# Where a two-layer encoder kernel makes its precomputed weight sums

## The reference, cut to what matters

```python
# layer 0 (even): neighbourhood attention heads || convolution channels
h = rmsnorm(x);  z = h @ w_in_e                      # q k v g_a u_a u_b g_b
a = neighbourhood_attention(q, k, v, rpb) * silu(g_a)          # 8 heads
u = conv31(u_a * sigmoid(u_b)) + dw_b
u = silu(layernorm(u)) * silu(g_b)
x = x + rmsnorm(concat(a, u) @ w_out_e)
x = x + sigmoid(x @ w_ple_gate[0]) * (p[0] @ w_ple[0])
# layer 1 (odd): latent attention heads || 2-D Fourier channels
h = rmsnorm(x);  z = h @ w_in_o                      # c_q c_kv k_rope g_c f g_d
...
```

## Time and profile before

| | us |
|---|---|
| median of three runs | 1905.9 |
| the profiled execution's own time | 1906.77 |
| its span in the profile | 1905.0 |
| PE busy | 1842.9 (97%) |
| DVE busy | 1339.1 (70%) |
| POOL busy | 858.5 (45%) |
| ACT busy | 800.9 (42%) |

### The profile page before, as it was taken

How to read it: one execution, slowest core, us unless ns; L and a number is a source line. 1 busy time by engine, 2 the same in 40 slices (tenths; PEclk the granted TensorE clock), 3 DMA queues, 4 the chain that set the end, 5 groups by cost and what they waited for, 6 DMA issues and landing times. The chain is left out here.

```text
span 1905.0 us, 27049 instructions
## 1 busy us (share of the span) xinstructions
PE 1842.9 (97%) x9736; PEld 1565.9 (82%) x9736; DVE 1339.1 (70%) x2021; ACT 800.9 (42%) x1581; POOL 858.5 (45%) x568
## 2 busy tenths in 40 slices
PE   6999999989999999998999999999999999999999
PEld 5888888868799888786888888887898998888887
DVE  5599999936688425621569966675777776788886
ACT  6211211211388432211245453432788787445432
POOL 2251341342488563365546241223788874354211
PEclk9999999999999999998999999999999999999999
DMA  5112452573387556555433343495546557657744
GB/s 202 45 45 103 159 157 67 172 241 108 119 276 245 183 192 222 193 181 176 163 124 120 127 145 101 159 359 170 161 144 203 184 187 295 236 177 278 267 143 139
DMA packets 160107, 331.93 MB, mean 174 GB/s; under 512 B 32690, under 2 KB 66226, under 8 KB 159987
## 3 DMA queue, kind: packets, MB, share of 16 engines
q1 hardware_dynamic: 159986, 330.36, 50.9%
HBM read 207.63 MB, written 122.68 MB: 173 GB/s over the span
## 5 line engine op out<-in xcount | busy, mean ns | idle before, releaser
L191 POOL TENSOR_TENSOR w_lo_part<-w_raw,w_hi_part 128x1024 fp32r<-128x1024 f32 x56 | 152.8, 2737 | 362.4 <-ACT w_hi_part L183 342.7
L605 DVE SCALAR_TENSOR_TENSOR ie_acc<-ie_u,ie_wconv,ie_acc 128x1551 f32<-128x1551 f32 x120 | 262.9, 2191 | 3.1
L3449 PE MATMUL og_ps<-w_hi_part,bl_ring 128*128 128x512 f32 x672 | 216.6, 393 | 1.0 <-DVE bl_ring L2982 1.0
L245 PE MATMUL ie_ps<-rows_hi,w_hi_part 128*128 128x512 f32 x384 | 151.1, 393 | 0.4 <-DVE ie_stage L619 0.4
L245 PE MATMUL ie_ps<-rows_lo,w_hi_part 128*128 128x512 f32 x384 | 149.7, 390 | 0.0
L245 PE MATMUL ie_ps<-rows_hi,w_lo_part 128*128 128x512 f32 x384 | 149.6, 389 | 0.0
L3449 PEld LDWEIGHTS og_ps<-w_hi_part,bl_ring 128*128 128x128 f32 x672 | 126.2, 188 | 26.8 <-DVE bl_ring L2982 1.1
L2870 DVE TENSOR_TENSOR mla_pt_lo<-mla_ps_t,mla_pt_hi 128x512 fp32r<-128x512 f32 x160 | 108.8, 686 | 33.0 <-ACT mla_pt_hi L2839 32.0
L3449 PE MATMUL og_ps<-w_lo_part,bl_ring 128*128 128x512 f32 x336 | 130.8, 389 | 0.0
L2863 DVE TENSOR_REDUCE mla_min<-mla_ps_s 128x1 f32<-128x1024 f32 (+1 forms) x96 | 99.9, 1042 | 29.5 <-PE mla_ps_s L2780 28.0
L2839 ACT CAST mla_pt_hi<-mla_ps_t 128x512 fp32r<-128x512 f32 x160 | 94.2, 590 | 60.7 <-PE mla_ps_t L2790 57.2
(11 more groups left out here) (361 smaller groups left out, 5242.3 us busy)
## 6 DMA issues: line engine op xcount, KB each, us to landing
w_raw<-wall SPq DMA_DIRECT2D x62, 512.0 KB, 4.7
w_hi_part<-weight_blocks SPq DMA_DIRECT2D x28, 512.0 KB, 4.6
w_lo_part<-weight_blocks SPq DMA_DIRECT2D x28, 512.0 KB, 5.9
weight_blocks<-w_hi_part SPq DMA_DIRECT2D x26, 512.0 KB, 6.3
w_raw_tiles<-wall SPq DMA_DIRECT2D x16, 512.0 KB, 5.5
odd_sums<-w_raw_tiles SPq DMA_DIRECT2D x8, 1024.0 KB, 4.3
w_raw<-odd_sums SPq DMA_DIRECT2D x16, 512.0 KB, 4.1
w_flat<-wall SPq DMA_DIRECT2D x16, 512.0 KB, 8.8
```

The costliest lines, as they stand in the source:

```text
L191: pool.tensor_tensor(g.W[1][:, pair % 2, off:off + QCOLS], g.raw[:, n % 2, :], g.W[0][:, pair % 2, off:off + QCOLS].bitcast(F32), ALU.subt ...
L245: mm = pe.matmul(psum[:, u % banks], w_at(g, name, a, k * HALF + c * P, P), g.XT[m][:, k, b * 512:(b + 1) * 512], start=i == 0, stop=i == ...
L605: dve.scalar_tensor_tensor(acc[:], ubuf[:, cc, s:s + CW], wconv[:, cc, s:s + 1], acc[:], ALU.mult, ALU.add).then_inc(taps, 1)
L3449: mm = pe.matmul(ps[:, N % 4], bl.part(a, N)[:, k], wb.at(N // HT, m, k), start=k + a + m == 0, stop=k == 3 and a == 1)
```

## The change: what it does

Slices 0, 1 and 2 are made in in_even at units 54, 66 and 69 (before: slices 0 to 4 at 18, 30, 42, 54 and 65). Slices 3 to 7 are made in natten, one beside each of heads 1 to 5 on POOL, and none in gate. In in_even the quarters for q, v and k are loaded at units 0, 2, 4, 6 of the block before and rounded at 2, 4, 6, 8 (before: 0, 0, 2, 3 and 1, 2, 3, 4). In in_odd S1 and S4 are made by POOL and no longer by DVE. The semaphores of `OddSums` now belong to those that gate clears.

```diff
-    SUM_LOADS = [18, 30, 42, 54, 65]
+    LOAD_AT = {"k": (0, 0, 2, 3), "ga": (0, 0, 2, 3)}
+    HIGH_AT = {"u0": (7, 8, 9, 10), "k": (1, 2, 3, 4), "ga": (1, 2, 3, 4)}
+    SUM_LOADS = [54, 66, 69]
...
-                if i + 1 < PIDX["out0_a"] and ((0, 2, 4, 6) if i == 0 else (0, 0, 2, 3))[q] == j:
+                if i + 1 < PIDX["out0_a"] and LOAD_AT.get(n, (0, 2, 4, 6))[q] == j:
...
-            at = (7, 8, 9, 10) if i == 0 else (1, 2, 3, 4)
+            at = HIGH_AT.get(names[i], (2, 4, 6, 8))
...
             for h in range(HEADS):
+                if 1 <= h < 6:
+                    os.store(sp, h + 2)
+                if h < 5:
+                    os.load(sp, h + 3, QBASE[PIDX["out0_a"]])
                 if h + 2 < HEADS:
                     load_xt(h + 2)
...
-                    os.wait_stored(sp, os.EARLY)
+                    os.wait_stored(sp, os.SLICES)
...
                 split_v(h)
+                if 1 <= h < 6:
+                    os.first_sums(pool, h + 2)
+                    os.second_sums(pool, h + 2)
...
-                if u in (8, 10, 12):
-                    os.store(sp, os.EARLY + (u - 8) // 2)
-                if u in (6, 8, 10):
-                    os.load(sp, os.EARLY + (u - 6) // 2, QBASE[PIDX["o7_0"]])
-                if u == 13:
-                    os.wait_stored(sp, os.SLICES)
...
-                if u in (7, 9, 11):
-                    os.first_sums(pool, os.EARLY + (u - 7) // 2)
-                    os.second_sums(pool, os.EARLY + (u - 7) // 2)
...
+                elif i == 2:
+                    sum_s1(j)
+                elif i == 3:
+                    sum_s4(j)
...
-                if 13 <= N < 13 + HT:
-                    sum_s1(N - 13)
-                if 19 <= N < 19 + HT:
-                    sum_s4(N - 19)
```

More of the change, by code:

```diff
@@ L1520, in out_proj, with gate @@
         g.end()
-def gate(g, l, ple, od, os, spent):
+def gate(g, l, ple, od, spent):
     nc = g.nc
@@ L1833 @@
 class OddSums:
-    SLICES, EARLY = 8, 5
+    SLICES = 8
     def __init__(self, g):
         self.g = g
-        self.raw_in, self.summed, self.stored = [g.nc.alloc_semaphore(name="os_" + n) for n in ("raw_in", "summed", "stored")]
+        self.raw_in, self.summed, self.stored = g.sem("os_raw_in"), g.sem("os_summed"), g.sem("os_stored")
     def load(self, sp, s, w_ready):
@@ L2043, in rms, with sum_s4, sum_s1 @@
             rms_scale(pool, g, ss[:, t, :], 1, pooled, 2 * t)
+        def sum_s4(j):
+            pool.wait_ge(sums["S2"], j + 1)
+            pool.tensor_tensor(od.block("S4", j), od.block("A12", j), od.block("S2", j), ALU.subtract).then_inc(sums["S4"], 1)
+        def sum_s1(j):
+            pool.wait_ge(sums["S3"], j + 1)
+            pool.tensor_tensor(od.block("S1", j), od.block("A21", j), od.block("A22", j), ALU.add).then_inc(sums["S1"], 1)
         for N in range(ODD_UNITS):
@@ L2147, in sum_s2 @@
             dve.tensor_tensor(od.block("S2", j), od.block("A22", j), od.block("S3", j), ALU.subtract).then_inc(sums["S2"], 1)
-        def sum_s1(j):
-            dve.wait_ge(sums["S3"], j + 1)
-            dve.tensor_tensor(od.block("S1", j), od.block("A21", j), od.block("A22", j), ALU.add).then_inc(sums["S1"], 1)
-        def sum_s4(j):
-            dve.wait_ge(sums["S2"], j + 1)
-            dve.tensor_tensor(od.block("S4", j), od.block("A12", j), od.block("S2", j), ALU.subtract).then_inc(sums["S4"], 1)
         def consume(N):
@@ L3538, in even_layer @@
             out_proj(g, 0, rows, ple)
-            gate(g, 0, ple, od, os, spent)
+            gate(g, 0, ple, od, spent)
         def odd_layer():
```

## The result

The changed kernel takes 1936.8 us (median of 4 runs, 1932.2 to 1941.3) against 1906.3 for the kernel before beside it on the same chip: the ratio is 1.0152, with an interval of 1.0134 to 1.0172. It is slower by 30 us. The forecast was 1916, with a range up to 1928: the direction was right, the size was not. The profiled execution took 1936.4 us for a span of 1934.6, so the comparison of the two traces covers 29.6 us.

A forecast was written before the change was run, and what follows sets the result against it. PE, busy 97% of the span, was taken to bound the kernel. Gate -11.9, in_even +5.3, natten +17 and in_odd 0 sum to +10.4 us, told as 1916 us, with 1900 to 1928 for 8 times in 10.

The forecast's parts named there:

- Gate: In gate, PE's 7.4 us of waits for POOL and 4.5 us of half clock go: -11.9 us.
- in_even: In in_even, two slices on POOL ahead of the first table delay tile 0 and the stage's end: +5.3 us.
- The upper bound: In in_even, the most it could lose: +11.5 us, if SP comes no earlier than now (6.4 more).
- +17, by the DMA rows: In natten, a head's transfers need 19.0 us against 15.6, 3.4 too much over five heads: +17 us.
- SP's chain: In natten, a slice's load 6.1, sums 5.3 and store 4.3 total 15.7 us and fit a head; lower end +5.
- The DMA's term: In natten, a slice's load 3.3 and store 3.5 take 6.8 us of all DMA engines, on top of 0.78.
- where SP's chain sets the pace PE's half speed is hidden in it: In natten, PE's half clock after waits adds nothing of its own to the +17 us.
- in_odd: In in_odd, PE is always busy and POOL has room for the sums: 0 us, bounds -0.5 and +3.
- and others don't: Port rule for natten: only DVE operations with two SBUF inputs and GpSimd block each other, so sums stay 5.3 us.
- the queue chokes: Rival: every natten head from 3 to 7 late, +24 or more, in_even +8: 1927 us; chance 0.15.
- The three others: Rivals: natten absorbs the slices, 1901 (0.20); natten +5 to +10, 1906, or no effect on PE, +0 to 3 (together 0.15).
- The forecast's own tests: Forecast wrong if natten still takes 131 us to its end, or if in_even ends before 511.

The follow-up runs named there:

- short sums: Changed kernel with POOL summing only 64 of 512 columns of slices 3 to 7 in natten; 1933.2 us, ratio 1.0156.
- short loads: Changed kernel with slices 3 to 7 loaded with 64 of 512 columns, sums and stores whole; 1921.4 us, ratio 1.0092.
- six and two: Kernel before with six slices in in_even, two in natten, none in gate, in_odd's sums on DVE; 1899.9 us, ratio 0.9965.
- sums on DVE: Changed kernel with in_odd's S1 and S4 back on DVE; 1925.8 us, ratio 1.0108.
- slices last: Changed kernel with natten's slice stores and next slice loads issued behind the coming head's table, keys, queries and values; 1967.9 us, ratio 1.0313.

## Why the prediction was wrong

**Gate: right.** -11.9 was forecast, -12.0 measured. PE's wait at L1731 is gone, no other stands behind it, and the 4.5 us of half clock came back with it.

**in_even: right, and by its own steps.** +5.3 forecast, +4.7 measured; in brackets what was measured of each step. Convolution rows issued at 411.8 (410.1), store 412.3 (410.6), sums of the second slice 423.6 (423.7), table 428.9 (429.0), tile 0 435.5 (435.2). The wait at the first turn was to be 1 to 2 and was 1.15, the one before unit 72 was to be 8 to 10 and was 9.9. The upper bound was added up wrong (5.3 + 6.4 is 11.7, not 11.5), with no effect.

**natten: the step that failed.** "+17, by the DMA rows"; it is +28.3. The step took the DMA engines' work for the pace of the late heads, 3.4 us too much for each, and held that SP's chain "fits a head". In its place the traces show a chain of 21.6 us from a store's issue to the landing of the next head's queries, and heads that are late by 8.2, 5.4, 9.2 and 5.4 us. The kind of wait was right: at the first score matmul of heads 3 to 6, ended by keys and queries. Of three parts of the working two were off and the third held. How the 28 us divide between the transfers' own time and the standing at a store's landing stays open.
- The chain was the wrong one. "Load 6.1, sums 5.3, store 4.3 = 15.7" leaves out the head's own loads and takes in the sums. The one that sets the start of the late heads is store, landing, slice load, table, keys, queries, landing: 21.6 us for head 3. The sums are beside it (short sums: 22.4), the slice's load is in it (short loads: 17.3). The landings that I took from the earlier trace rows, 4.3 and 5.5, were medians over quiet stages; in natten they are 6.5 and 6.3.
- The DMA's term, from which I took the 17, was too large for what it stands for. I had 6.8 us a slice from the stretches of the earlier trace rows, which hold other traffic too; measured are 5.7 (changed) and 5.8 (six and two). A head's transfers take 0.78 x 15.6 + 5.7 = 17.9 and not 19.0, 2.3 more than a head, 11.5 for five. That the forecast came as near as 17 is owed to this error.
- "where SP's chain sets the pace PE's half speed is hidden in it": the trace bears this out. The heads from 3 to 6 start when their queries land, whatever PE did before, and SP's issues did not wait for PE: the keys of head 4, issued at 578.1, needed the scores of head 2, done at 560.6. From the start of head 6 to the last score it is 29.4 us, as in the kernel before (602.6 to 632.0 there, 635.6 to 665.0 here). So the 8 us that PE is busy longer lie in time that would else have been idle, and the 28.3 are the late landings alone.

**in_odd: failed.** "0, bounds -0.5 and +3 (a late S4)"; it is +5.5. I asked only if POOL had time and if its results came in time. I did not ask what POOL's operation does to DVE, which in this stretch was busy 79.3 of 80 us: an engine without any slack, and its small operations on the rope read SBUF alone. The runs show the price: 0.18 us becomes 1.3 beside one of the sums. The 2.4 beside a split of the weights was there before. The Trainium skill ("SBUF — State Buffer", "SBUF: two separate sides") says that a GpSimd operation and a DVE one with two SBUF inputs, or in a mode with two ports, exclude each other for a whole operation. The runs agree, here and in natten, where DVE's large operations read PSUM and the sums took 5.3 us each. I had weighed that rule for natten alone, and had told it too short: with "and others don't" the mode with two ports was left out, and DVE's 128x128 operation with a scalar, which has one SBUF input, took 1.33 us in place of 0.28.

**What was left out.** out_proj and the hand-over to it, +3.7: the clock stands at half from 672.0 to 682.2, behind natten's end. natten's lateness is not shown to be the cause: "sums on DVE" has the same natten (150.3 us), full clock in these same 10 us and 160.8 us of out_proj, and "short loads" and "slices last" keep full clock there too. Why the clock fell in this execution is open.

The rivals: of "the queue chokes", every head from 3 on late and natten +24 or more, natten's part came true; its in_even did not. The three others fell. The forecast's own tests said that it would be wrong if natten still took 131 us; it failed at the other end, for which the range had only that rival.

## What to carry to other kernels

Work put on an engine that runs in order is tied to everything behind it there: before a transfer with its consumer goes into a full stage, follow both queues, the one that issues it and the one that waits for it, issue the load behind the stage's own and ahead of what waits for the same engine, and leave two turns between the load and its use. Here these two together made the difference between 126.3 and 172.7 us for three slices. When a wait is forecast for PE, add the half clock behind it at its full price, as in gate, unless the next thing on PE waits for something that PE's speed doesn't move, as the heads in natten did. And before work goes from DVE to POOL, look at what DVE runs beside it: where DVE is full, an operation of POOL's with two SBUF operands costs DVE time even if POOL has time to spare and nobody reads the result.

## What the runs showed of the hardware

- A DVE operation on SBUF alone can last as long as POOL's operation beside it: 128x32 elements took 0.18 us alone, 1.30 beside a POOL operation of 1.3 us and 2.38 beside the split of 128x1024 (2.4 us and more), and 128x128 with a scalar (one SBUF input) 0.28 and 1.33. With a PSUM operand one of 128x512 stayed at 0.67.
- A store of 1 MB that lands in 4.3 us in the median of the kernel before takes 6.5 in natten, and where it was issued 4.3 us earlier it landed 0.9 earlier: the transfers queued ahead of it decided more than its own issue did.
- Two slices of 2 MB of traffic each went through natten at a DMA share of 0.87 without a wait of PE's; five at 0.82 cost 28 us. The share alone did not tell which would fit.
